# Two transformer blocks on one core: the modulation weights load through GpSimd's DMA queue instead of the sync engine's

## The chip, the core and the metric

The kernel runs on one NeuronCore of a Trainium2 chip. A core has TensorE for matrix products, VectorE (DVE in the profile) and ScalarE (ACT) for element-wise work, GpSimd (POOL), and the sync engine (SP). Each has its own instruction queue, and they wait for each other only through semaphores. Transfers between the chip's memory (HBM) and the on-chip buffer run on 16 DMA engines. They are issued from the queue of the sync engine, of ScalarE or of GpSimd. The metric is the device time of one execution in microseconds; less is better.

## What is computed

A sequence of 256 tokens of width 2048 goes through two blocks in float32. The first is a mixer layer (RG-LRU, mLSTM and block attention side by side) with cross attention to a memory of 256 tokens. The second has two layers, a pooling branch and a latent attention branch (MLA), both modulated by two condition vectors. What matters here is this modulation, and that everything else is products with large weights, each used once:

```python
for i in range(DEPTH_2):                       # 2 layers
    shift, scale, gate = jnp.split(jax.nn.silu(c) @ ada_w[i] + ada_b[i], 3, axis=-1)
    h_lat = rms_norm_2(x, pre_norm[i]) * (1 + scale[:, None]) + shift[:, None]
    shift_c, scale_c, gate_c = jnp.split(jax.nn.silu(c_ctx) @ ada_w[i] + ada_b[i], 3, axis=-1)
    h_ctx = rms_norm_2(ctx, pre_norm[i]) * (1 + scale_c) + shift_c
    ...
    x = x + gate[:, None] * rms_norm_2(y_lat, post_norm[i])
```

`ada_w` is 2 x 2048 x 6144 in float32, 100 MB of the 307 MB that the kernel reads. It is multiplied with two vectors only, and none of it depends on the tokens.

## The kernel before

**The weight products.** Every weight product is an object `Product`: a weight in *chunks* of 512 rows by up to 512 columns (`KC` = 4 row tiles of 128, 1 MB), in column groups. There are 196 chunks in all. A chunk goes through four hands: the sync engine loads it into one of two buffers `raw` (`sp_chunk`, L253), ScalarE rounds it into a high part (`act_high`, L302, `w_high`), VectorE subtracts that from it into a low part (`dve_low`, L312, `w_low`), and TensorE multiplies high and low parts with the operand (`pe_chunk`, L497 to L499 for one sequence of 256 columns, L506 to L508 for two sequences, 512 columns). 48 matrix instructions belong to a full chunk. Buffers are in pairs, so chunk c + 2 may be loaded once VectorE has made the low part of chunk c (`lo_ready`).

**The modulation weights.** `ada_w` is loaded in 192 *units* of 512 rows by 256 columns, 512 KB each and 1 KB a row, into one of two buffers `ada_raw` (`sp_unit`, L267). VectorE multiplies a unit with both condition vectors and adds it up in `ada_acc` (`dve_ada`): eight instructions a unit, one for each of 4 row tiles and 2 vectors, L427, or L423 for the first two of a block. Four units are a block; then TensorE collects the sums (`pe_ada`, L441 or L444), and VectorE waits for that before it overwrites them. Unit u + 2 may be loaded when unit u is summed: the issue waits for `ada_link`, which every one of the eight instructions raises.

**How units are spread.** The units have no own place in time. They are handed out to the chunks of some products (the dictionary `ada`), so that VectorE sums them while TensorE multiplies:

```python
ada = {kv: 1, win_a: 1, win_c: 1, mixo: 1, xq: 1, xo: 1, po: 2}
ada.update({p: 1 for p in pu})
ada.update({p: 2 for p in pgate + uq + ukv})
```

`kv`, `win_a`, `win_c`, `mixo`, `xq` and `xo` are products of one sequence with one unit a chunk, 80 units. The `pu` products have two sequences and one unit a chunk, 16 units. The four `pgate` products and `po` have two sequences and two units a chunk, 64 units. The last 32 units belong to the *pairs*, the eight pairs of attention heads of the MLA layer (`uq0` and `ukv0` to `uq7` and `ukv7`, two units each). `win_b`, `cq`, `mg01`, `ckv`, `kr`, `mg23` (together the stage `latents` with the operands' normalisation) and the last product `mo` have none. In `dve_product` and its like the order on VectorE is: low part of chunk j, what the former group left, units of chunk j, low part of chunk j + 1.

**The sync engine's queue** is what the change touches. `sp_group` issues chunk j, then the units of chunk j, then chunk j + 1. Each issue waits at its place, and everything behind it waits too. Ahead of the first product stand the four loads of the memory tokens (`sp_turn`, L611). For the pairs `sp_pairs` has a written-out order. GpSimd has no work in the kernel. The kernel's head reserves 1024 bytes of each partition for descriptors of GpSimd's transfers: `nc = bacc.Bacc("TRN2", target_bir_lowering=False, num_devices=1, dynamic_dma_scratch_size=1024)`. ScalarE's queue issues some thirty small loads of vectors at the start, and the tokens of the other inputs.

The stages follow each other with a wait of all three compute engines for one another (`stage_end`, L790).

Of the kernel before, what the change touches and what calls it, by code (L numbers as in the profile page):

```python
# [21 lines left out]
DEBUG_STOP = None  # L22
# [102 lines left out]
def build(nc, a, out):  # L125
# [24 lines left out]
    uq = [Product(f"uq{j}", mw_uq, 1, 1, 3, 1, "copy1", half=1, width=384, pack="heads", col0=384 * j, dest=Q_SETS[j % 2], banks=4)  # L150
          for j in range(8)]
    ukv = [Product(f"ukv{j}", mw_ukv, 1, 1, 4, 2, "copy2", src="ps", col0=GW * j, dest=KV_SETS[j % 2], banks=4) for j in range(8)]
    mo = Product("mo", mw_out, 4, 4, 4, 1, "gain1", dest=32, banks=6)
    pool_chain = [pu[3], pu[2], pg[3], pu[1], pg[2], pu[0], pg[1], pgate[3], pg[0], pgate[2], pgate[1], pgate[0], po]
    products = [kv, win_a, win_b, win_c, mixo, xq, xo] + pool_chain + [cq, mg01, ckv, kr, mg23]
# [16 lines left out]
    with ctx:  # L172
        def sb(name, shape, dt=F32):
            return ctx.enter_context(nc.sbuf_tensor(name, shape, dt))

        def sem(name):
            return ctx.enter_context(nc.semaphore(name))
# [14 lines left out]
        ARAW = sb("ada_raw", [P, 2, KC, 256])  # L192
# [5 lines left out]
        for name, _, n in VEC:  # L198
            if at % P + n > P:
                at += P - at % P  # L200
            V[name], place[name] = PV[:, at:at + n], at
            at += n
# [18 lines left out]
        ada_loaded = [sem("ada_loaded0"), sem("ada_loaded1")]  # L221
        ada_summed, rows_moved, rows_turned = sem("ada_summed"), sem("ada_rows_moved"), sem("ada_rows_turned")
        rows_added = sem("ada_last_rows_added")
        ada_link = sem("ada_link")
# [16 lines left out]
        block = ctx.enter_context(nc.Block())  # L241


        def sp_chunk(sp, p, i, j):
            c, w = p.chunk0 + j, p.chunks * i
            if isinstance(i, int):
                c, w = c + w, 0
            slot = c % 2
            if c >= 2 or not isinstance(i, int):
                sp.wait_ge(lo_ready, c + w - 1)  # L250
            rows = p.w[p.korder[j] * KC * P:(p.korder[j] + 1) * KC * P, :]
            src = rows.rearrange("(k p) n -> p k n", p=P)[:, :, bass.ds(p.col0 + p.stride * i, p.width)]
            sp.dma_start(RAW[:, slot, :, 0:p.width], src).then_inc(raw_ready[slot], 16)  # L253

        def sp_unit(sp, p, i, j, q):
            u0 = p.unit0 + p.ada * j + q
            uw = p.ada * p.chunks * i
            if isinstance(i, int):
                u0, uw = u0 + uw, 0
            part, us = u0 % 4, u0 % 2  # L260
            if u0 >= 2 or not isinstance(i, int):
                sp.wait_ge(ada_link, 8 * (u0 + uw - 1))
            b = u0 // 4
            layer, col = b // 24, (b % 24) * 256
            src = a["ada_w_2"][layer, part * KC * P:(part + 1) * KC * P, :]
            src = src.rearrange("(k p) n -> p k n", p=P)[:, :, bass.ds(col, 256)]
            sp.dma_start(ARAW[:, us], src).then_inc(ada_loaded[us], 16)  # L267

        def sp_group(sp, p, i):
            for j in range(p.chunks):  # L270
                sp_chunk(sp, p, i, j)
                for q in range(p.ada):
                    sp_unit(sp, p, i, j, q)

        def packed(p):

# [249 lines left out]
        def sp_product(sp, p):  # L526
            sp_group(sp, p, 0)
            if p.groups > 1:
                for g in range(1, p.groups):
                    sp_group(sp, p, g)  # L530
# [77 lines left out]
        def sp_turn(sp, q, src):  # L608
            for part in range(4):
                cols = slice(512 * part, 512 * (part + 1))  # L610
                sp.dma_start(tok(q)[:, :, cols], src[:, cols].rearrange("(a p) f -> p a f", p=P)).then_inc(tok_in[part], 16)  # L611
# [1429 lines left out]
        def sp_pairs(sp):  # L2041
            sp_chunk(sp, uq[0], 0, 0)
            sp_chunk(sp, ukv[0], 0, 0)
            for j in range(8):
                if j < 7:
                    sp_chunk(sp, uq[j + 1], 0, 0)
                sp_unit(sp, uq[j], 0, 0, 0)
                if j < 7:
                    sp_chunk(sp, ukv[j + 1], 0, 0)
                sp_unit(sp, uq[j], 0, 0, 1)  # L2050
                sp_unit(sp, ukv[j], 0, 0, 0)
                sp_unit(sp, ukv[j], 0, 0, 1)


        out_t, out_c = sem("out_turned"), sem("out_copied")
# [60 lines left out]
        def sp_out(sp):  # L2116
            for n in range(8):
                k4, h = n // 2, n % 2
                sp.wait_ge(out_c, n + 1)
                sp.dma_start(out[0, h * P:(h + 1) * P, 512 * k4:512 * (k4 + 1)],  # L2120
                             OUTT[:, h, 512 * k4:512 * (k4 + 1)]).then_inc(out_done, 16)
            sp.wait_ge(out_done, 16 * 8)
# [34 lines left out]
        @block.sync  # L2157
        def _(sp):
            sp_turn(sp, 0, a["mem"][0])
            sp_product(sp, kv)  # L2160
            for p in products[1:3]:
                sp_product(sp, p)
            if DEBUG_STOP:
                lim = STAGES.index(DEBUG_STOP)
            else:
                lim = len(STAGES)
            for p in products[3:]:
                if p in uq[1:] + ukv:
                    continue
                stage = ("pools" if p in pool_chain else "latents" if p in (cq, mg01, ckv, kr, mg23) else "pairs" if p is uq[0]  # L2170
                         else stage_of.get(p.name, p.name))
                if STAGES.index(stage) >= lim:
                    break
                if p is uq[0]:
                    sp_pairs(sp)
                    continue
                sp_product(sp, p)
            if not DEBUG_STOP:
                sp_out(sp)

        @block.scalar
        def _(act):
# [154 lines left out]
```

## Time and profile before

| | |
|---|---|
| runs shown | 2194.4, 2195.2, 2198.5 us; median 2195.2 |
| profiled execution | 2198.2 us, span 2196.4 us |
| TensorE busy | 1864.9 us, 85% of the span |
| VectorE busy | 1521.2 us, 69% |
| ScalarE busy | 778.0 us, 35% |
| GpSimd busy | 0.2 us |
| read from HBM | 307.2 MB, 141 GB/s over the span |
| transfers of the sync engine's queue | 303.6 MB, 42.2% of 16 engines' span |
| granted TensorE clock | 0.907 of full speed on average |

The profiled execution is one of its own, 3.0 us above the median of the runs. In the profile a line such as L267 is a line of the kernel. `SPq` is the sync engine issuing transfers: the time there is that of the issue, and the landing is given apart. A wait of an engine is put down to what came last before it went on.

### The profile page before, as it was taken

The page shows a single profiled execution, that of the slowest core. Times are in us where ns is not written, and L with a number is a line of the kernel's source. Part 1 is how long each engine was busy: PE and PEld are TensorE (multiplying, and loading weights), DVE is VectorE, ACT ScalarE, POOL GpSimd, SP SyncE. Part 2 cuts the span into 40 slices and gives each one's busy share as a digit, 9 for nine tenths or more (in the row PEclk, how much of TensorE's full clock was granted, in tenths as well). Part 3 has the DMA queues.
Part 4 walks back from the last instruction along what each step waited for, and adds up shares of the span by engine and source line. Part 5 has one row for each costly group of instructions (what it writes and reads, how often), then busy time and mean ns, then how long its engine had stood idle before and what let it go on. Part 6 is the DMA issues. An engine that isn't in the chain of part 4 may idle for free.

```text
span 2196.4 us, 27206 instructions
## 1 busy us (share of the span) xinstructions
PE 1864.9 (85%) x10672; PEld 1582.7 (72%) x10672; DVE 1521.2 (69%) x2851; ACT 778.0 (35%) x1048; POOL 0.2 (0%) x4
## 2 busy tenths in 40 slices
PE   3969960769979967569999999999688989999797
PEld 2969950559958966458888877777587886666497
DVE  3778966378858866468668787978765277887444
ACT  4343342223333243532233222222443344444243
POOL 0000000000000000000000000000000000000000
PEclk8979975669989987879999999999799999999798
DMA  3748830038735734024445444555243343342153
GB/s 122 250 127 257 262 112 1 1 95 264 254 102 189 252 115 142 31 97 134 134 135 167 159 154 153 192 172 185 85 137 102 122 153 125 106 139 82 66 174 115
DMA packets 214780, 311.10 MB, mean 142 GB/s; under 512 B 11528, under 2 KB 118392, under 8 KB 214652
## 3 DMA queue, kind: packets, MB, share of 16 engines
q1 hardware_dynamic: 207104, 303.59, 42.2%
q10 hardware_dynamic: 7548, 5.78, 0.9%
q8 instruction: 84, 1.38, 0.3%
q14 instruction: 44, 0.36, 0.1%
HBM read 307.23 MB, written 2.10 MB: 141 GB/s over the span
## 4 chain that ended last, share of the span: by engine, by line
PE 53%; DVE 11%; ACT 3%; issue 1%; DMA 0%; DVEq 0%; ACTq 0%
PE bank L506 10%; PE bank L507 10%; PE bank L508 10%; PE bank L497 5%; PE bank L499 5%; PE bank L498 5%; DVE ada_acc L427 3%; DVE w_low L312 2%; PE bank L1838 2%; ACT w_high L302 2%; PE bank L672 2%; PE bank L1837 1%; PE bank L441 1%; DVE big L700 1%; PE bank L1857 1%
## 5 line engine op out<-in xcount | busy, mean ns | idle before, releaser
L497 PE MATMUL bank<-operand,w_high 128*128 128x256 f32 x2000 | 583.7, 292 | 80.3 <-DVEq L790 55.0
L312 DVE TENSOR_TENSOR w_low<-raw,w_high 128x2048 fp32r<-128x2048 f32 (+4 forms) x208 | 437.2, 2107 | 271.6 <-ACT w_high L302 269.7
L302 ACT ACTIVATE w_high<-raw 128x2048 fp32r<-128x2048 f32 (+4 forms) x208 | 366.0, 1765 | 645.0 <-PE bank L499 274.0
L427 DVE SCALAR_TENSOR_TENSOR ada_acc<-ada_raw,silu_c,ada_acc 128x256 f32<-128x256 f32 x1440 | 584.0, 482 | 1.8 <-DMA ada_raw<-in_ada_w 0.5
L498 PE MATMUL bank<-operand,w_high 128*128 128x256 f32 x2000 | 575.4, 288 | 0.0
L499 PE MATMUL bank<-operand,w_low 128*128 128x256 f32 x2000 | 575.1, 288 | 0.0
L497 PEld LDWEIGHTS bank<-operand,w_high 128*128 128x128 f32 x2000 | 394.0, 197 | 103.1 <-ACTq L790 45.2
L498 PEld LDWEIGHTS bank<-operand,w_high 128*128 128x128 f32 x2000 | 394.1, 197 | 0.1
L499 PEld LDWEIGHTS bank<-operand,w_low 128*128 128x128 f32 x2000 | 393.5, 197 | 0.0
L506 PE MATMUL bank<-operand,w_high 128*128 128x512 f32 x784 | 309.7, 395 | 29.7 <-DVEq L790 28.3
L507 PE MATMUL bank<-operand,w_high 128*128 128x512 f32 x784 | 307.0, 392 | 0.0
L508 PE MATMUL bank<-operand,w_low 128*128 128x512 f32 x784 | 306.4, 391 | 0.0
L506 PEld LDWEIGHTS bank<-operand,w_high 128*128 128x128 f32 x784 | 148.1, 189 | 69.4 <-ACTq L790 28.7
L508 PEld LDWEIGHTS bank<-operand,w_low 128*128 128x128 f32 x784 | 148.0, 189 | 31.4
L507 PEld LDWEIGHTS bank<-operand,w_high 128*128 128x128 f32 x784 | 148.2, 189 | 30.2
L506 PE MATMUL bank<-operand_small,w_high 128*128 128x512 f32 x256 | 103.6, 405 | 3.5 <-DVE big L406 3.5
L508 PE MATMUL bank<-operand_small,w_low 128*128 128x512 f32 x256 | 100.4, 392 | 0.0
L507 PE MATMUL bank<-operand_small,w_high 128*128 128x512 f32 x256 | 100.4, 392 | 0.0
L346 ACT ACTIVATE big<-bank 128x256 f32<-128x256 f32 x91 | 34.6, 380 | 98.8 <-PE bank L499 98.1
L672 PE MATMUL bank<-big,ones 128*128 128x256 f32 x192 | 52.6, 442 | 16.8 <-ACT big L651 16.8
L506 PEld LDWEIGHTS bank<-operand_small,w_high 128*128 128x128 f32 x256 | 48.5, 189 | 18.6 <-DVE w_low L312 5.3
L672 PEld LDWEIGHTS bank<-big,ones 128*128 128x128 f32 x192 | 42.8, 226 | 25.5 <-issue 10.0
(296 smaller groups left out, 1619.7 us busy)
## 6 DMA issues: line engine op xcount, KB each, us to landing
ada_raw<-in_ada_w SPq DMA_DIRECT2D x192, 512.0 KB, 3.9
raw<-in_w_in SPq DMA_DIRECT2D x48, 1024.0 KB, 5.1
raw<-in_pool_w_in SPq DMA_DIRECT2D x32, 1024.0 KB, 5.6
raw<-in_mla_w_in SPq DMA_DIRECT2D x24, 1024.0 KB, 5.1
raw<-in_w_out SPq DMA_DIRECT2D x16, 1024.0 KB, 5.8
raw<-in_pool_w_out SPq DMA_DIRECT2D x16, 1024.0 KB, 6.2
raw<-in_mla_w_out SPq DMA_DIRECT2D x16, 1024.0 KB, 5.1
raw<-in_xa_wkv SPq DMA_DIRECT2D x8, 1024.0 KB, 6.9
```

The lines of the kernel that those rows point to most:

```text
L302: ins = nc.scalar.activation(view(HI, slot, False), view(RAW, slot, True), ACT.Copy)
L312: ins = nc.vector.tensor_sub(view(LO, slot, False), view(RAW, slot, True), view(HI, slot, False).bitcast(F32))
L346: nc.scalar.activation(dest_ap(p, i, n), PB[p.bank[i, n]][:, 0:T], ACT.Copy).then_inc(act_freed, 1)
L427: ins = nc.vector.scalar_tensor_tensor(ACC[:, v], ARAW[:, us, k], SC[:, v, part * KC + k:part * KC + k + 1], ACC[:, v], ALU.mult, ALU.add)
L497: pe.matmul(bank[:, 0:T], pick(HI), x[:, 0, :], start=first, stop=False, skip_group_check=True)
L498: pe.matmul(bank[:, 0:T], pick(HI), x[:, 1, :], start=False, stop=False, skip_group_check=True)
L499: ins = pe.matmul(bank[:, 0:T], pick(LO), x[:, 0, :], start=False, stop=last, skip_group_check=True)
L506: pe.matmul(bank[:, :], pick(HI), x[:, 0, :], start=first, stop=False, skip_group_check=True)
L507: pe.matmul(bank[:, :], pick(HI), x[:, 1, :], start=False, stop=False, skip_group_check=True)
L508: ins = pe.matmul(bank[:, :], pick(LO), x[:, 0, :], start=False, stop=last, skip_group_check=True)
L672: ins = pe.matmul(PB[5][:, 0:T], ones[:, :], BIG[:, SQ0 + 4 * (s % 2) + k, :], start=(s == 0 and k == 0), stop=(s == n["nk"] // 4 - 1 and ...
L1838: la_pe.inc(pe.matmul(bank[:, :], BIG[r, q_of(a)[2], qt * P:(qt + 1) * P], KRT[r, :], start=False, stop=True), "s", a, u)
```

## The change

The units' loads leave the sync engine's queue and go to GpSimd's, in the same order, with the same waits for `ada_link` and the same landing semaphores. GpSimd does nothing else. The sync engine's queue keeps the chunks. Nothing is changed on TensorE, VectorE and ScalarE.

```diff
--- before.py
+++ after.py
@@ -252,25 +252,23 @@
             src = rows.rearrange("(k p) n -> p k n", p=P)[:, :, bass.ds(p.col0 + p.stride * i, p.width)]
             sp.dma_start(RAW[:, slot, :, 0:p.width], src).then_inc(raw_ready[slot], 16)
 
-        def sp_unit(sp, p, i, j, q):
+        def pool_unit(pool, p, i, j, q):
             u0 = p.unit0 + p.ada * j + q
             uw = p.ada * p.chunks * i
             if isinstance(i, int):
                 u0, uw = u0 + uw, 0
             part, us = u0 % 4, u0 % 2
             if u0 >= 2 or not isinstance(i, int):
-                sp.wait_ge(ada_link, 8 * (u0 + uw - 1))
+                pool.wait_ge(ada_link, 8 * (u0 + uw - 1))
             b = u0 // 4
             layer, col = b // 24, (b % 24) * 256
             src = a["ada_w_2"][layer, part * KC * P:(part + 1) * KC * P, :]
             src = src.rearrange("(k p) n -> p k n", p=P)[:, :, bass.ds(col, 256)]
-            sp.dma_start(ARAW[:, us], src).then_inc(ada_loaded[us], 16)
+            pool.dma_start(ARAW[:, us], src).then_inc(ada_loaded[us], 16)
 
         def sp_group(sp, p, i):
             for j in range(p.chunks):
                 sp_chunk(sp, p, i, j)
-                for q in range(p.ada):
-                    sp_unit(sp, p, i, j, q)
 
         def packed(p):
 
@@ -2044,12 +2042,8 @@
             for j in range(8):
                 if j < 7:
                     sp_chunk(sp, uq[j + 1], 0, 0)
-                sp_unit(sp, uq[j], 0, 0, 0)
                 if j < 7:
                     sp_chunk(sp, ukv[j + 1], 0, 0)
-                sp_unit(sp, uq[j], 0, 0, 1)
-                sp_unit(sp, ukv[j], 0, 0, 0)
-                sp_unit(sp, ukv[j], 0, 0, 1)
 
 
         out_t, out_c = sem("out_turned"), sem("out_copied")
@@ -2178,6 +2172,16 @@
             if not DEBUG_STOP:
                 sp_out(sp)
 
+        @block.gpsimd
+        def _(pool):
+            for p in products:
+                if DEBUG_STOP:
+                    break
+                for i in range(p.groups):
+                    for j in range(p.chunks):
+                        for q in range(p.ada):
+                            pool_unit(pool, p, i, j, q)
+
         @block.scalar
         def _(act):
             for name, st in all_steps:
```

What stands in the queues where the prediction looks: first the sync engine's, before the change, at the start of `po` (`in_pool_w_out`; `in_ada_w` are the units).

```order
L253 DMA raw<-in_pool_w_in 128x4x512 [waits lo_ready]
L267 DMA ada_raw<-in_ada_w 128x4x256 [waits ada_link] x2
L253 DMA raw<-in_pool_w_out 128x4x512 [waits lo_ready]
L267 DMA ada_raw<-in_ada_w 128x4x256 [waits ada_link] x2
L253 DMA raw<-in_pool_w_out 128x4x512 [waits lo_ready]
L267 DMA ada_raw<-in_ada_w 128x4x256 [waits ada_link] x2
```

And the same queue before, where the pairs begin (`in_mla_w_uq` and `in_mla_w_ukv` are the chunks of `uq` and `ukv`):

```order
L267 DMA ada_raw<-in_ada_w 128x4x256 [waits ada_link] x2
L253 DMA raw<-in_mla_w_in 128x4x512 [waits lo_ready] x16
L253 DMA raw<-in_mla_w_in 128x4x64 [waits lo_ready] x4
L253 DMA raw<-in_mla_w_in 128x4x512 [waits lo_ready] x8
L253 DMA raw<-in_mla_w_uq 128x4x384 [waits lo_ready]
L253 DMA raw<-in_mla_w_ukv 128x4x512 [waits lo_ready]
L253 DMA raw<-in_mla_w_uq 128x4x384 [waits lo_ready]
L267 DMA ada_raw<-in_ada_w 128x4x256 [waits ada_link]
L253 DMA raw<-in_mla_w_ukv 128x4x512 [waits lo_ready]
L267 DMA ada_raw<-in_ada_w 128x4x256 [waits ada_link] x3
L253 DMA raw<-in_mla_w_uq 128x4x384 [waits lo_ready]
L267 DMA ada_raw<-in_ada_w 128x4x256 [waits ada_link]
```

The sync engine's queue with the change, from the last `pgate` products to the pairs:

```order
L253 DMA raw<-in_pool_w_in 128x4x512 [waits lo_ready] x12
L253 DMA raw<-in_pool_w_out 128x4x512 [waits lo_ready] x16
L253 DMA raw<-in_mla_w_in 128x4x512 [waits lo_ready] x16
L253 DMA raw<-in_mla_w_in 128x4x64 [waits lo_ready] x4
L253 DMA raw<-in_mla_w_in 128x4x512 [waits lo_ready] x8
L253 DMA raw<-in_mla_w_uq 128x4x384 [waits lo_ready]
L253 DMA raw<-in_mla_w_ukv 128x4x512 [waits lo_ready]
L253 DMA raw<-in_mla_w_uq 128x4x384 [waits lo_ready]
L253 DMA raw<-in_mla_w_ukv 128x4x512 [waits lo_ready]
L253 DMA raw<-in_mla_w_uq 128x4x384 [waits lo_ready]
```

The units are gone from between the chunks; at the pairs they had stood behind chunks of `uq1` and `ukv1`. GpSimd's queue with the change, whole:

```order
L2331 MEMSET const-float32-0.0 128x1
L2331 MEMSET const-float32-1.0 128x1
L2331 MEMSET const-bfloat16-1.0 128x1
L2331 MEMSET const-uint8-127 128x1
L2175 UNCONDITIONAL_BRANCH [waits barrier_Pool_Activation_PE_DVE_SP_gather]
L267 DMA ada_raw<-in_ada_w 128x4x256 x2
L267 DMA ada_raw<-in_ada_w 128x4x256 [waits ada_link] x190
L172 UNCONDITIONAL_BRANCH
```

All 192 units stand there in a row; only the first two wait for nothing.

## Rows read from the trace of the kernel before

**Rows 1.** The page: the span, busy us, share and instructions of each engine
```profile
span 2196.4 us, 27206 instructions
...
PE 1864.9 (85%) x10672; PEld 1582.7 (72%) x10672; DVE 1521.2 (69%) x2851; ACT 778.0 (35%) x1048; POOL 0.2 (0%) x4
```

**Rows 2.** TensorE's waits: us in total, times, longest
```profile
PE bank L753 <- DMA small<-in_ml_bf: 18.4, 1, 18.4
PE bank L497 <- DVE w_low L312: 18.4, 10, 4.2
...
PE bank L444 <- DVE ada_acc L427: 3.2, 1, 3.2
```

**Rows 3.** Busy us by stretch: inside `win_a`, `mixo` and `po`
```profile
core 0: us, PE busy (x) PEld busy (x) DVE busy (x) ACT busy (x) POOL busy (x), PEclk, DMA share, GB/s
150.00:280.00 130.00, 130.00 (x1057) 126.42 (x1056) 116.94 (x196) 47.25 (x42) 0.00 (x0) 1.00 0.79 251
...
680.00:755.00 75.00, 75.00 (x606) 72.63 (x606) 69.44 (x124) 23.53 (x13) 0.00 (x0) 1.00 0.78 253
...
1400.00:1540.00 140.00, 140.00 (x610) 111.73 (x609) 113.16 (x222) 38.60 (x48) 0.00 (x0) 1.00 0.55 188
```

**Rows 4.** Chunk loads in 150:280, inside `win_a`: xcount, ns, first and last start
```profile
L253 SPq DMA_DIRECT2D raw<-in_w_in x22: 367/368/368, 151.2 to 278.0; - x22
```

**Rows 5.** The unit buffer, whole span: xcount, ns min/median/max, first and last start
```profile
L427 DVE SCALAR_TENSOR_TENSOR ada_acc<-ada_raw,silu_c,ada_acc x1440: 474/481/503, 55.0 to 2043.4; 128x256 f32<-128x256 f32 x180
L267 SPq DMA_DIRECT2D ada_raw<-in_ada_w x192: 367/368/2982, 4.0 to 2033.5; - x192
...
DMA to landing us min/median/max: 3.4/3.9/13.0
```

**Rows 6.** The unit buffer in 1404:1527, inside `po`
```profile
L267 SPq DMA_DIRECT2D ada_raw<-in_ada_w x22: 367/368/368, 1405.1 to 1525.8; - x22
...
  PE bank L441: 18.2, 5
...
DMA to landing us min/median/max: 3.8/3.9/5.0
```

**Rows 7.** The sync engine's queue at the start of `po`: start, us, instruction
```profile
1349.70 0.51 SPq L253 DMA_DIRECT2D raw<-in_pool_w_out  x1
1376.93 3.54 SPq L267 DMA_DIRECT2D ada_raw<-in_ada_w  x2
1380.51 0.51 SPq L253 DMA_DIRECT2D raw<-in_pool_w_out  x1
```

**Rows 8.** ScalarE's waits for chunks, whole span: us, times, longest
```profile
ACT w_high L302 <- DMA raw<-in_pool_w_out: 46.1, 5, 18.5
ACT w_high L302 <- DMA raw<-in_pool_w_in: 40.1, 4, 12.1
```

**Rows 9.** VectorE in `po`, in order of time
```profile
1484.17 5.63 DVE L427 SCALAR_TENSOR_TENSOR ada_acc<-ada_raw,silu_c,ada_acc 128x256 f32<-128x256 f32 x14
1489.71 2.29 DVE L312 TENSOR_TENSOR w_low<-raw,w_high 128x2048 fp32r<-128x2048 f32 x1
1491.92 6.43 DVE L427 SCALAR_TENSOR_TENSOR ada_acc<-ada_raw,silu_c,ada_acc 128x256 f32<-128x256 f32 x16
```

**Rows 10.** The chain that ended last, at the start of the pairs: start, us, what
```profile
1804.64 3.27 DVE ada_acc L427 x8
...
1807.92 3.69 DMA ada_raw<-in_ada_w
...
1811.64 3.27 DVE ada_acc L427 x8
...
1814.95 1.06 PE bank L444 x4
```

**Rows 11.** The sync engine's queue in the first 22 us
```profile
0.73 2.36 SPq L611 DMA_DIRECT2D big<-in_mem  x4
...
6.36 2.98 SPq L267 DMA_DIRECT2D ada_raw<-in_ada_w  x1
```

## Prediction

> **What bounds the kernel now.** I read the page first, then TensorE's waits, then the busy time of single stretches, then the two weight buffers, and last the chain of waits where the pairs begin. The page has TensorE busy for 85% of the span and GpSimd with nothing to do [rows 1]. Inside the weight products TensorE does not pause at all: 130.00 of 130.00 us in `win_a`, 75.00 of 75.00 in `mixo`, 140.00 of 140.00 in `po`, at a granted clock of 1.00 [rows 3]. So there a load can only cost time, not give any back. What VectorE has free is little: 13 of 130 us in `win_a`, 5.6 of 75 in `mixo`, 27 of 140 in `po`. TensorE's waits for a weight's low part are 18.4 us in ten places, and one wait of 3.2 us is for a modulation sum [rows 2]. No wait of TensorE names a chunk or unit load.
>
> A unit lands 3.9 us after its issue in the middle case, 3.4 at best, 13.0 at worst (the first ones) [rows 5]. VectorE needs 8 instructions of some 0.4 us step for a unit, 3.27 us together [rows 10].
>
> **The change, part by part.**
>
> *Taken from the sync queue: 192 issues of 0.37 us* [rows 5]. In the 1-sequence products a chunk goes out every (278.0 - 151.2) / 21 = 6.04 us [rows 4]. Its issue waits for the low part of the chunk two before; the unit issues ahead of it wait for sums that VectorE makes before that low part. So the chunks don't go out earlier there: 0 us. In the products with two units a chunk the queue does hold chunks back. At the start of `po` the sync engine issues a chunk at 1349.70, stands until 1376.93 before the next pair of units, and issues the next chunk at 1380.51 [rows 7]. ScalarE waits 46.1 and 40.1 us for such chunks [rows 8]. The change takes most of these 86 us away, and I cost that at 0: TensorE is busy for every microsecond of that stretch [rows 3], and VectorE and ScalarE only prepare the next chunk sooner. What is late next is TensorE itself.
>
> *Added: 192 loads on GpSimd's queue.* GpSimd waits for nothing but the unit buffer, and nothing else is queued on it. The cost is a unit's latency there, which this trace does not show. From below it is the best unit load of the sync queue, 3.4 us; from above, the 6.2 us that I get when the median load first waits out a VectorE subtraction of 2.29 us [rows 5, 9]. I take 4.4, the median 3.9 and one more issue time of 0.5 [rows 7], since it is the same transfer on the same DMA engines. By the Trainium skill, "DMA: Bandwidth & Descriptors", section "Anatomy of one DMA — SWDGE (gpsimd) path", such a load takes 2.0 us and its bytes at 436 GB/s, which for 512 KB makes 3.2 us, an estimate from that page alone; by it the term of the pairs, below, would be 2 x 3.2 - 7.0 = -0.6 us. The second unknown is how many loads GpSimd's queue holds. The sync queue takes two in a row [rows 7]. The kernel reserves only 1024 bytes of a partition for GpSimd's descriptors, so I take one at a time, and two as the other end.
>
> *Where the latency is covered.* In the 1-sequence products a buffer comes free when a unit is summed, and its successor is due two chunks later less one sum: 2 x 6.04 - 3.27 = 8.8 us against 4.4. One load per chunk also fits one at a time, as long as it takes under 6.04. In `po` the sequence is unit, unit, low part (2.29), unit, unit [rows 9]. A load is due 3.2 + 2.3 = 5.5 us after its request. With 4.4 the first of a pair is in time, and the second, which starts when the first has landed, comes 2 x 4.4 - 3.2 = 5.6 after its own request: VectorE waits 0.1 us. That vanishes in the 18.2 us which VectorE waits there for TensorE at five block starts [rows 6]. Sum: 0.
>
> *Where it is not covered: the start of the pairs* [rows 10]. The first two units there land long before use (the sync queue gave them only at the end of `latents`). The third is requested at 1804.6 when the first is summed, the fourth at 1807.9. Now the chain runs 1807.92 + 3.69 us of load, then 3.27 us of sums, then TensorE at 1814.95, which had waited 3.2 us [rows 2]. With 4.4 us, one at a time, the third lands at 1809.0, the fourth at 1813.4, and its sums end at 1816.7: 1.8 us later. With two in flight it is 1812.3 + 3.3 = 1815.6: 0.7 us later. In later pairs steps of the attention stand between the sums on VectorE, and all four loads stay covered.
>
> *The start of the kernel.* The first two unit loads now stand behind 2 MB of tokens and two chunks [rows 11]; from GpSimd they compete from the first microsecond. TensorE's first work waits for the small vectors at 18.4 us [rows 2], which end together with all this traffic. The bytes are the same, so 0. The two units are 1 MB of some 6, a sixth of 18 us, so the ends are 3 us either way.
>
> **Sum:** 0 + 0 + 0 + 1.8 + 0 = +1.8 us. The profiled execution took 2198.2 us, 3.0 above the median of the runs shown; from it I get 2200.0, from the median 2195.2 + 1.8 = 2197.0. A measurement of this kernel can tell about 0.2%, 4.4 us, from no change.
>
> **The rivals.**
>
> *GpSimd's loads are slow (slower, 15%).* In `po` a unit is due every (1525.8 - 1405.1) / 21 = 5.75 us [rows 6]. With one load at a time this is the point from which it decides: a latency above 5.75 makes the loads the bound of the 32 chunks with two units (64 units), and above 6.04 of the 80 units of the 1-sequence products too. At 6.0 us it costs 64 x 0.25 = +16 us (2211); at the 6.2 of a load that waits out a subtraction 64 x 0.45 + 80 x 0.16 = +42 (2237); at 6.5, 64 x 0.75 + 80 x 0.46 = +85 (2280). For it: loads beside chunks are slower on the sync queue too, up to 5.0 in `po` [rows 6]. Against it: the median there is 3.9, so GpSimd would have to add half again. The Trainium skill bears on it, in "SBUF — State Buffer", sections "SBUF: two separate sides" and "Who interferes with whom": GpSimd cannot write descriptors while VectorE holds the port pair they share. By that page a subtraction of two tensors takes only the read side and does not starve them; no row here shows either.
>
> *VectorE itself is slowed by GpSimd (slower, 10%).* In `win_a` VectorE has 13 us free for 21 units, in `mixo` 5.6 for 10: about 0.6 us a unit. Only what a load takes beyond that reaches TensorE. With 1.0 us it is 80 x 0.4 = +32 us (2229); with one blocked sum of 0.48 us nothing. Nothing in the trace speaks for it, as GpSimd is idle.
>
> *A middling latency (10%).* Between 5.0 and 5.75 us each second unit in `po` and the gates comes 1.3 to 2.8 us late. Blocks mostly absorb it; I price it with the pairs (2 x 5.5 - 7.0 = +4.0) at +3 to +8 us (2198 to 2203).
>
> *The earlier requests pay (5%).* Units and chunks that no longer wait for each other cut the kernel's start by up to 3 us and some of the 18.4 us of waits for low parts [rows 2]: -5 us, 2190. Against it: most of those ten waits lie in products without units.
>
> **How the numbers follow.** The forecast, loads absorbed but for 1.8 us, has 60%. The range takes in it (2194 to 2200), the early gain's near part, the middling latency and the low ends of both slow rivals: 2192 to 2213 leaves out about 0.2. Slower by over 0.2% is 0.15 + 0.10 and most of the middling case, 0.32; faster 0.05; the same 0.63.
>
> **What would show it.** In the profile of the changed kernel: GpSimd's queue with 192 loads and a median to landing near 4.4 us; the sync queue without its stands; ScalarE's 86 us of waits for chunks nearly gone; TensorE still busy for all of the three stretches; at the pairs, the fourth sum's end 1 to 2 us later relative to its first. A median above 5.75, waits of VectorE for units in `win_a`, or sums longer than 0.48 us each would show the forecast wrong.

## The result, and the profile after

| | before | after | ratio |
|---|---|---|---|
| median, 10 runs each | 2195.83 us (2194.38 to 2198.54) | 2201.38 us (2196.8 to 2203.28) | 1.0024 [1.0014, 1.0034] |
| profiled execution | 2198.22 us, span 2196.4 | 2201.21 us, span 2199.4 | |

The change makes the kernel slower by 0.24%, about 5.3 us. The forecast was 2197.0 us, +1.8 against the median shown then. The range of 2192 to 2213 us holds the result, but the case given the highest chance, no change beyond 0.2%, was missed by a little. The two profiled executions lie only 3.0 us apart, because that of before was 2.4 us above its median.

The page of the changed kernel first: the span, the engines, and two of the lines on DMA queues. The last row is of the page of before.

```profile
span 2199.4 us, 27206 instructions
...
PE 1868.2 (85%) x10672; PEld 1585.6 (72%) x10672; DVE 1520.9 (69%) x2851; ACT 778.3 (35%) x1048; POOL 145.0 (7%) x196
...
q1 hardware_dynamic: 105728, 202.91, 28.0%
q0 software_dynamic: 27648, 100.68, 14.0%
```

```profile
q1 hardware_dynamic: 207104, 303.59, 42.2%
```

VectorE and ScalarE do the same work [rows 1]. GpSimd is now busy for 145 us, all of it issuing. The columns of the queue lines are packets, MB, and the share of 16 engines' time. The 100.68 MB of the units took 207104 - 105728 = 101376 packets (1 KB each) on the sync engine's queue and take 27648 (3.6 KB on average) on GpSimd's.

The unit buffer over the whole span, in the changed kernel (answers to [rows 5]):

```profile
L425 DVE SCALAR_TENSOR_TENSOR ada_acc<-ada_raw,silu_c,ada_acc x1440: 469/477/487, 55.4 to 2044.9; 128x256 f32<-128x256 f32 x180
L267 POOL DMA_DIRECT2D ada_raw<-in_ada_w x192: 748/753/887, 1.3 to 2035.4; - x192
...
  DMA ada_raw<-in_ada_w: 24.2, 16
...
DMA to landing us min/median/max: 3.8/4.3/8.1
```

A unit lands 4.3 us after its issue in the middle case; 4.4 was taken. A sum takes 477 ns at the median (481 before), so VectorE is not slowed by GpSimd. New is the third line: VectorE stands 24.2 us, in 16 places, for units that haven't landed. In the three stretches TensorE is still busy throughout (answers to [rows 3]; columns as there):

```profile
150.00:280.00 130.00, 130.00 (x1057) 126.42 (x1056) 115.80 (x192) 46.77 (x41) 15.82 (x21) 1.00 0.79 256
680.00:755.00 75.00, 75.00 (x607) 72.66 (x606) 69.71 (x124) 23.00 (x12) 9.04 (x12) 1.00 0.77 250
1400.00:1540.00 140.00, 140.00 (x611) 111.68 (x610) 109.76 (x217) 38.71 (x48) 18.58 (x25) 1.00 0.56 181
```

The waits of the changed kernel that answer to [rows 2, 8] (us in total, times, longest):

```profile
ACT w_high L300 <- DMA raw<-in_w_in: 29.2, 7, 4.9
ACT w_high L300 <- DMA raw<-in_w_out: 26.1, 6, 5.0
PE bank L751 <- DMA small<-in_ml_bf: 18.7, 1, 18.7
PE bank L495 <- DVE w_low L310: 16.6, 10, 4.2
PE bank L442 <- DVE ada_acc L425: 5.1, 1, 5.1
PE bank L439 <- DVE ada_acc L425: 3.7, 1, 3.7
```

ScalarE's 86 us of waits for `pool_w_out` and `pool_w_in` chunks are gone, as forecast. Other chunks are waited for instead, those of the one-sequence products. TensorE's wait for a sum at the pairs has grown from 3.2 to 5.1 us. The last line is a second wait of TensorE for a sum. The prediction counted one such wait in the kernel before, but there were two. Its rows left this one out:

```profile
PE bank L441 <- DVE ada_acc L427: 4.2, 1, 4.2
```

**Where it is.** The chain of waits runs through both places. This is the chain of before at the start of `po`, then that of after at the same place:

```profile
1379.99 2.50 DVE operand L931 x4
1382.48 2.83 DVE ada_acc L427 x8
1385.56 3.27 DVE ada_acc L427 x8
1388.87 1.49 PE bank L441 x4
```

```profile
1374.33 3.27 DVE ada_acc L425 x8
1377.60 1.94 issue
1379.54 4.36 DMA ada_raw<-in_ada_w
1383.92 3.27 DVE ada_acc L425 x8
1387.24 1.94 PE bank L439 x4
```

Before, VectorE makes the four sums of `po`'s first block one after the other, and TensorE waits for the last. After, the chain passes through a load and through 1.94 us in which GpSimd could have issued but did not. VectorE in the changed kernel shows what that costs:

```profile
1379.91 3.25 DVE L425 SCALAR_TENSOR_TENSOR ada_acc<-ada_raw,silu_c,ada_acc 128x256 f32<-128x256 f32 x8
1383.92 3.26 DVE L425 SCALAR_TENSOR_TENSOR ada_acc<-ada_raw,silu_c,ada_acc 128x256 f32<-128x256 f32 x8 [0.77 <-DMA ada_raw<-in_ada_w]
```

At the pairs the same thing happens (the chain of after; answers to [rows 10]), with GpSimd's own timeline below it:

```profile
1804.05 3.26 DVE ada_acc L425 x8
1807.31 1.60 issue
1808.91 4.00 DMA ada_raw<-in_ada_w
1812.94 3.27 DVE ada_acc L425 x8
1816.25 1.94 PE bank L442 x4
```

```profile
1804.53 0.75 POOL L267 DMA_DIRECT2D ada_raw<-in_ada_w  x1 [254.64 <-DVE ada_acc L425]
1808.91 0.76 POOL L267 DMA_DIRECT2D ada_raw<-in_ada_w  x1 [3.63 <-issue]
```

The fourth unit's buffer is free at 1807.31, but its load starts at 1808.91. The third unit landed at 1808.6, 0.3 us earlier. So one load is in flight at a time here, as the prediction took it, and by issue and landing no two of the 192 loads overlap in this profile. From the start of the second unit's sums (1804.05) to the end of the fourth's (1816.21) it is 12.16 us. Before it was 1804.64 to 1814.91, 10.27 us [rows 10]. The difference is 1.9 us, and 1.8 was forecast. The match is partly luck. The two loads took 4.1 and 4.0 us, less than the 4.4 that was taken. But each also starts late: the third unit's 0.4 us after its buffer was free, the fourth's 0.3 us after the third landed. Neither delay was in the sum. Together it is 8.8 us, as 2 x 4.4.

So the one priced term was right, and yet 5.3 us are measured. The open question for the runs is what the other 3.5 us are.

### The profile page after: what moved, and what is told of

Its sections match the earlier page's. It is cut to its first block, busy times and chain, and to the rows that moved or that the text cites. A ratio compares the mean times of both kernels' runs of the same rounds, so it can differ in the third digit from the quotient of the medians.

```text
span 2199.4 us, 27206 instructions
## 1 busy us (share of the span) xinstructions
PE 1868.2 (85%) x10672; PEld 1585.6 (72%) x10672; DVE 1520.9 (69%) x2851; ACT 778.3 (35%) x1048; POOL 145.0 (7%) x196
## 3 DMA queue, kind: packets, MB, share of 16 engines
q1 hardware_dynamic: 105728, 202.91, 28.0%
q0 software_dynamic: 27648, 100.68, 14.0%
## 4 chain that ended last, share of the span: by engine, by line
PE 54%; DVE 10%; ACT 3%; issue 2%; DMA 1%; DVEq 0%; ACTq 0%
PE bank L504 10%; PE bank L505 10%; PE bank L506 10%; PE bank L495 5%; PE bank L496 5%; PE bank L497 5%; DVE ada_acc L425 2%; DVE w_low L310 2%; PE bank L1836 2%; ACT w_high L300 1%; PE bank L670 1%; PE bank L1835 1%; PE bank L439 1%; PE bank L1855 1%; DVE big L698 1%
## 5 line engine op out<-in xcount | busy, mean ns | idle before, releaser
L425 DVE SCALAR_TENSOR_TENSOR ada_acc<-ada_raw,silu_c,ada_acc 128x256 f32<-128x256 f32 x1440 | 584.7, 478 | 25.5 <-DMA ada_raw<-in_ada_w 24.2
L267 POOL DMA_DIRECT2D ada_raw<-in_ada_w x192 | 144.8, 754 | 1890.9 <-DVE ada_acc L425 1672.6
```

The source lines that it names most:

```text
L267: pool.dma_start(ARAW[:, us], src).then_inc(ada_loaded[us], 16)
L425: ins = nc.vector.scalar_tensor_tensor(ACC[:, v], ARAW[:, us, k], SC[:, v, part * KC + k:part * KC + k + 1], ACC[:, v], ALU.mult, ALU.add)
```

## The experiments

Two theories. **W:** the cost is TensorE's waits for modulation sums where four of them follow each other, and comes from one load at a time. **C:** it is spread over the one-sequence products, whose chunk loads became slower. The expectations below also use the letter P for W's place at the pairs. They speak of a wait at "the end of `po`". That was misread: by the chain above it is at `po`'s start, in its first block. Ratios are to the kernel before on the same chip.

**1. The change once more, unaltered, and 2. with more space for descriptors.**

> The changed kernel once more, unaltered, to see which differences of the two profiles repeat. Theory P (the cost sits at the pairs: loads of units come one at a time, so the fourth sum of the pairs is late): the kernel is 4 to 6 us above the one before, TensorE's wait for the fourth sum is about 5.1 us again (3.2 before), and the step of +2 us at the start of the pairs is there again. Theory C (the cost is spread over the one-sequence products, where chunk loads got slower beside GpSimd's units, 6.4 to 6.9 us instead of 5.1 to 5.8): the time is the same, but small steps stand in win_a, win_c and mixo, and TensorE's waits for low parts grow. Steps of the first comparison that are noise (about -2.4 at the start of the gates, +1.4 at po, -3.0 and +2.4 in the latents) change size or sign here.

Measured: 2202.30 us, ratio 1.0030 [1.0018, 1.0041]. TensorE's waits for sums are 5.0 us at `po` and 4.9 at the pairs; in this order they are given for the other runs too. The differences of 1 to 3 us that the expectation called noise did change sign or size, and waits for low parts are 19.3 us (18.4 before).

```diff
-dynamic_dma_scratch_size=1024
+dynamic_dma_scratch_size=1536
```

> Only the space for GpSimd's descriptors grows, from 1024 to 1536 bytes of a partition. Theory 1 (the space holds one unit's descriptors, so the next load waits for the landing of the last): with half as much again there is at best part of a second unit in flight; if it holds two, no load starts 0.31 us after a landing, VectorE's waits for units fall from 24 us to under 8, the fourth sum of the pairs is 1 us earlier and the kernel 1 us shorter than the changed one. Theory 2 (GpSimd's queue takes one transfer at a time whatever the space): nothing moves, VectorE waits 24 us again, the time is 5 us above the kernel before.

Measured: 2197.10 us, ratio 1.0008 [0.9999, 1.0016]. GpSimd at the pairs in this run, and the waits for units and sums of the whole span, TensorE's first:

```profile
1801.43 0.76 POOL L267 DMA_DIRECT2D ada_raw<-in_ada_w  x1 [259.37 <-DVE ada_acc L425]
1804.60 0.75 POOL L267 DMA_DIRECT2D ada_raw<-in_ada_w  x1 [2.41 <-DVE ada_acc L425]
```

```profile
  PE bank L442: 3.9, 1
...
  PE bank L439: 2.8, 1
  DVE ada_acc L425: 1.2, 1
...
DMA to landing us min/median/max: 3.8/4.2/9.8
```

The second load starts 3.17 us after the first, while that is still in flight, and the releaser is VectorE's sum and no longer "issue". VectorE's 24.2 us of waits for units fall to 1.2. With the latency nearly the same (4.2 against 4.3 us), two loads in flight take away about two thirds of the loss. Theory 1 stands: it was the space for descriptors, and theory 2 falls.

**3. and 4. The pairs apart.** The units of some products go back to the sync engine's queue at their old places. They raise semaphores of their own there (`ada_loaded_sp`). Only `on_pool` differs between these runs; it is shown for run 3, and run 4 has `p in uq + ukv`:

```diff
+        on_pool = lambda p: p not in uq + ukv
-            pool.dma_start(ARAW[:, us], src).then_inc(ada_loaded[us], 16)
+            pool.dma_start(ARAW[:, us], src).then_inc((ada_loaded if on_pool(p) else ada_loaded_sp)[us], 16)
```

> The 32 units of the pairs go back to the sync engine's queue at their old places, the other 160 stay with GpSimd. Theory P (the cost sits at the pairs): 0 to +1.5 us against the kernel before, TensorE's wait for the fourth sum 3.2 us again. Theory C (it is spread over the one-sequence products): still +3 to +4 us, and only the 2 us of the pairs' start go.

Measured: 2198.21 us, ratio 1.0012 [1.0003, 1.0021]. Waits 6.3 and 3.8 us. The wait at `po` is long because in this profile TensorE's clock did not fall ahead of it, so that TensorE comes to it sooner.

> The reverse: only the 32 units of the pairs go through GpSimd, the other 160 are issued by the sync engine as before. Theory P: +4 to +5 us against the kernel before. Theory C: +2 us, the late fourth sum alone.

Measured: 2198.17 us, ratio 1.0015 [1.0006, 1.0024]; the wait at the pairs is 5.2 us, at `po` 4.2. So the 32 units of the pairs alone cost 1.5/1000 or 3.3 us, where the late sum explains 1.9; without them 2.6 us remain. Neither theory is right as it stood: P had the whole cost at the pairs, C only 2 us of it.

**5. and 6. The other units apart**, with `on_pool` true for `(kv, win_a, win_c, mixo, xq, xo)` in 5, for `pu + pgate + [po]` in 6.

> Only the 80 units of the one-sequence products (kv, win_a, win_c, mixo, xq, xo) go through GpSimd; the 112 others stay with the sync engine. There is one unit a chunk here, so one load at a time is enough. Theory W (what the change costs is TensorE's waits for modulation sums at the end of po and at the pairs): same time as the kernel before, within 1 us, waits for sums 4.2 and 3.2 us as before. Theory C (chunk loads slowed by GpSimd's units cost time): +1 to +3 us; chunk loads of win_a and win_c take 6.4 to 7 us instead of 5.1 in either theory.

Measured: 2196.58 us, ratio 1.0005 [0.9997, 1.0014]. Waits 2.8 and 3.5 us.

> Only the 80 units of the gates and po (pu, pgate, po) go through GpSimd. Theory W: TensorE's wait for the last sums of po grows from 4.2 us to 5 or 6, the wait at the pairs stays at 3.2; the time is +1 to +2 us against the kernel before. Theory C: the same as before, since chunk loads of these products did not get slower (5.4 to 6.2 us in both).

Measured: 2198.07 us, ratio 1.0009 [1.0000, 1.0018]. The wait at `po` is 4.8 us, at the pairs 3.7. The three parts add up: 0.5 + 0.9 + 1.5 = 2.9 thousandths, against 2.4, 3.0 and 1.7 for the whole change in three comparisons. The 80 units of the one-sequence products, where one load a chunk needs no second one in flight, are the cheapest share and can't be told from nothing, though their chunk loads are slower there too. Chunk loads in 150:280 of this run:

```profile
DMA to landing us min/median/max: 4.9/6.2/7.6
```

The same line reads 4.4/5.0/7.2 for before and 4.2/6.7/8.0 for after. In the other runs with these units on GpSimd's queue it is 6.1 to 7.0 us. So C's fact is true and its cost is at most small: by the interval of this run, not above 1.4 thousandths.

**7. Each unit as two transfers of 256 KB, space left at 1024 bytes.**

```diff
-            pool.dma_start(ARAW[:, us], src).then_inc(ada_loaded[us], 16)
+            for h in range(2):
+                pool.dma_start(ARAW[:, us, 2 * h:2 * h + 2], src[:, 2 * h:2 * h + 2]).then_inc(ada_loaded[us], 16)
-                dve.wait_ge(ada_loaded[us], 16 * (u0 // 2 + 1) + 8 * uw)
+                dve.wait_ge(ada_loaded[us], 32 * (u0 // 2 + 1) + 16 * uw)
```

> The changed kernel with each unit as two transfers of 256 KB on GpSimd's queue, the space for descriptors left at 1024 bytes. If the space holds a number of descriptors and a whole unit takes over half of it, three halves fit: half of the next unit is in flight beside the last one, VectorE's waits for units fall from 20 to 24 us to under 10, and the time lies 1 to 3 us below the changed kernel. If a queue of GpSimd takes one transfer at a time, a unit takes two transfers in a row, some 6.5 us together, more than the 5.75 us in which one is due in po: +20 us or more.

Measured: 2197.62 us, ratio 1.0010 [1.0002, 1.0019]. GpSimd at the pairs:

```profile
1802.76 1.44 POOL L268 DMA_DIRECT2D ada_raw<-in_ada_w  x2 [257.85 <-DVE ada_acc L426]
1805.93 0.72 POOL L268 DMA_DIRECT2D ada_raw<-in_ada_w  x1 [1.73 <-DVE ada_acc L426]
1807.13 0.73 POOL L268 DMA_DIRECT2D ada_raw<-in_ada_w  x1 [0.48 <-issue]
```

Two halves go out together, then the third when the buffer is free, and the fourth waits 0.48 us for space. VectorE's waits for units are 9.1 us. So it isn't that the queue takes one transfer at a time: what is limited is how much is outstanding. A second kernel without the larger space confirms run 2, at twice the issues.

**8. Slow loads by hand.** The rival with the highest price, made by asking late, with no other work.

```diff
-                pool.wait_ge(ada_link, 8 * (u0 + uw - 1))
+                pool.wait_ge(ada_link, 8 * (u0 + uw - 1) + (4 if p.ada == 2 else 0))
```

> The changed kernel, but in the products with two units a chunk GpSimd asks for a unit only when four of the eight sums of the unit before it are made: 1.64 us later for 96 units, with no other work added. This is the rival of slow loads by hand. It says: a unit is then due every 0.4 + 4.4 + 1.6 = 6.4 us in po against the 5.75 it may take, 0.65 us over for 64 units, about +42 us; with what VectorE had free at block starts, +20 to +42. If the waits of VectorE at block starts swallow it, under +10.

Measured: 2286.29 us in one run, +90 us. The unit buffer in 1430:1560, inside `po`:

```profile
L267 POOL DMA_DIRECT2D ada_raw<-in_ada_w x19: 748/751/760, 1432.8 to 1555.4; - x19
...
  DMA ada_raw<-in_ada_w: 41.9, 18
...
DMA to landing us min/median/max: 4.2/4.4/5.1
```

A unit goes out every (1555.4 - 1432.8) / 18 = 6.8 us, not 6.4, because a low part often stands between the two sums it waits for. Against the 5.75 us of [rows 6] that is 1.06 us for each of the 32 units of `po`, 34 us; the trace has `po` 36 us longer than the kernel before, and 34 longer than the change in its first profile. Against the kernel before the gates are 25 us longer, and the pairs with the start of `mo` 29, which the expectation had left out. So a spacing above the 5.75 us costs what the rival says, the excess times the units. The expectation was too low twice: with 0.65 us a unit for 1.06, and by stopping at `po`. VectorE's free time at block starts swallows nothing of this.

**9. and 10. Both kernels again**, for the profiles.

> The kernel before, unaltered, as a second profile and as a comparison with itself. Ratio 1.000 within 0.001. TensorE's waits for modulation sums should be 4.2 and 3.2 us again, whereas the stretches in which its clock is granted at half speed should shift: if this profile has as much matrix work at half clock as the profiles of the variants (196 to 205 us) and not as they stand against the first profile (204), stages' differences of 1 to 3 us with equal waits are placed by the clock and not by the change.

Measured: 2195.04 us, ratio 1.0002 [0.9993, 1.0011]. Waits 4.2 and 3.9 us.

> The changed kernel a third time, beside the kernel before on this chip. Theory W: ratio 1.002 to 1.003; waits for sums at the end of po 3.7 to 5.0 us (4.2 before) and at the pairs 4.9 to 5.1 us (3.2 before), and the half-speed stretch behind the pairs' wait is 6.8 us long again, against 3.4 us in every variant in which that wait was 4.2 us or less. If it is 3.4 us here, the clock's part of the cost at the pairs is chance.

Measured: 2200.19 us, ratio 1.0017 [1.0008, 1.0025]. Waits 4.9 and 5.1 us.

**11. and 12. Towards a version below both.** Both have 1536 bytes; `on_pool` is that of run 6 in the first, that of run 3 in the second.

> An attempt at a version below both: the 80 units of the gates and po through GpSimd, with 1536 bytes for descriptors, all others by the sync engine. Theory W: the wait at the end of po falls from 4.2 to 2.8 us as in the run with the larger space, the pairs wait 3.2 to 3.7; -1.4 us, so 0.9985 to 1.0 of the kernel before, at the limit of what can be told. If sums that come earlier in po are worth nothing, 1.000 to 1.001.

Measured: 2195.77 us, ratio 1.0005 [0.9997, 1.0014]. Waits 4.2 and 3.4 us.

> The changed kernel with both remedies: 1536 bytes for descriptors, and the 32 units of the pairs by the sync engine. Theory W: no exposed wait is longer than before (2.8 at po, 3.2 to 3.8 at the pairs), so 0.999 to 1.0005 of the kernel before. If something else that goes with GpSimd's loads costs the rest (chunk loads of 6.4 to 7 us in the one-sequence products), 1.001 as in the run with the larger space alone.

Measured: 2196.36 us, ratio 0.9999 [0.9990, 1.0007]. Waits 4.2 and 3.9 us. Its chunk loads in the one-sequence products are waited for as in the change (ScalarE, 48.9 us for `in_w_in`), and it is as fast as before, to 0.7 thousandths by the interval. That ends theory C as an explanation. No version beats the kernel before: the 2.8 us at `po` that runs 2 and 5 showed is no gain, as the next table says.

**All profiles side by side.** The length of `po` and of the first exposed step of the pairs is that between the semaphore steps that tell a chunk as finished: the last of the gates to the last of `po`, and `ukv0`'s to `uq1`'s. "Busy" is TensorE's share of it.

| run | units by GpSimd, one at a time | `po` us (busy) | pairs step us (busy) |
|---|---|---|---|
| before | none | 195.17 (187.42) | 13.77 (10.53) |
| before again | none | 195.13 (187.37) | 14.37 (10.52) |
| one_seq_by_gpsimd | neither here nor there | 195.19 (188.90) | 13.96 (10.48) |
| ring_1536 | two at a time | 195.19 (188.90) | 14.39 (10.50) |
| half_units | more than one | 195.17 (187.40) | 14.77 (10.53) |
| gates_gpsimd_ring | two at a time in `po` | 195.17 (187.43) | 13.89 (10.48) |
| pairs_sync_ring | two at a time in `po` | 195.16 (187.42) | 14.43 (10.52) |
| two_seq_by_gpsimd | in `po` | 195.63 (187.27) | 14.24 (10.50) |
| pairs_by_sync | in `po` | 196.82 (186.99) | 14.33 (10.54) |
| pairs_by_gpsimd | in the pairs | 195.13 (187.41) | 15.97 (10.80) |
| after | in both | 197.29 (190.12) | 15.85 (10.72) |
| after again | in both | 195.87 (187.36) | 16.57 (11.63) |
| after, third | in both | 195.65 (187.19) | 16.76 (11.64) |

`po` is 195.13 to 195.19 us long in eight profiles, whatever TensorE's clock did in it, and 195.63 to 197.29 in the five with one load at a time: 1.1 us more on average. The pairs' step averages 14.1 us where the sync engine loads the pairs' units, and 16.3 in the four with one load at a time: 2.1 us more. No profile of one group lies in the other. The sum is 3.2 us. Where the wait at `po` was only 2.8 us (one_seq_by_gpsimd, ring_1536), TensorE was busy 1.5 us longer ahead of it at its lower clock, and the stage is as long as ever.

Both differences have two parts. At `po` TensorE goes on 28.45 us after the last chunk of the gates in all eight profiles, and 29.0 to 29.3 in the five: 0.5 to 0.9 us later, which is how long VectorE waits for the unit. In three of the five that is all. At the pairs TensorE goes on 6.0 to 6.6 us after `ukv0`'s chunk in the seven profiles, and 7.7 to 7.9 in the four: 1.45 us later on average. The rest in both places is the clock.

**The clock's share.** TensorE's granted clock after the pairs' wait, 10 us from the sums' collection on, in the second profile of after and then in the second of before (us, busy PE, PEld, DVE, ACT, POOL, PEclk, DMA share, GB/s):

```profile
1815.40:1825.40 10.00, 10.00 (x35) 5.97 (x36) 4.18 (x7) 3.47 (x6) 0.76 (x1) 0.71 0.18 58
```

```profile
1811.00:1821.00 10.00, 9.98 (x38) 5.73 (x39) 5.25 (x9) 4.29 (x7) 0.00 (x0) 0.83 0.01 2
```

With the shorter wait (3.9 us) 0.83 is granted, with the longer (4.9) 0.71: (0.83 - 0.71) x 10 = 1.2 us of work at full speed, and the busy column of the table has 1.1 more. The first profile of before has 0.83 too, and the third of after 0.71. The stretch at the lower level (1.2 GHz) at this wait is 3.4 us long in the nine profiles where the wait is 3.2 to 4.2 us, and 6.8 us in the four where it is 4.9 to 5.2. Even so the busy column has only 0.2 to 0.3 more in `after` and pairs_by_gpsimd: there the low stretch began some 3 us before TensorE went on, and fell in part on the wait itself. So the surcharge in the step is seen in two profiles of four. In these other two the chunk ahead of the step also took 10.0 and 9.1 us instead of 7.6, at the lower clock. The wait behind it can't have caused that. Whether the change did stays open.

At `po` the same is seen in two of the five, `after` and pairs_by_sync, whose stage is 2.1 and 1.7 us longer instead of 0.5 to 0.7. The 10 us from the sums' collection on, in the first profile of after and then in the third:

```profile
1387.20:1397.20 10.00, 9.96 (x31) 7.20 (x32) 10.00 (x20) 1.92 (x1) 1.51 (x2) 0.69 0.54 180
```

```profile
1387.50:1397.50 10.00, 9.97 (x37) 7.36 (x38) 10.00 (x20) 1.92 (x1) 1.51 (x2) 0.84 0.55 182
```

In the two the low stretch at this wait is 6.8 us long, in the other eleven 3.4. The length of the wait alone doesn't decide it. It was 3.7 and 6.3 us in the two, and 4.8 to 5.0 in the three that kept 3.4. What does decide is not shown.

## Why the prediction was right and wrong

- **Latency 4.4 us:** measured 4.3 from the issue on. What comes before the issue was left out: GpSimd's queue starts 0.40 us after the buffer is free, the sync engine's 0.03. The rule of the Trainium skill that was weighed against it ("DMA: Bandwidth & Descriptors", section "Anatomy of one DMA — SWDGE (gpsimd) path"; 3.2 us for 512 KB as an estimate from that page) is not borne out here: the best of 192 loads took 3.8 us.
- **One load at a time:** right, and the cause of most of the loss, since with two in flight the ratio falls from 1.0017 to 1.0030 to 1.0008.
- **Start of the pairs, +1.8 us:** the sums end 1.9 us later relative to the first. With two at a time +0.7 was forecast; the wait there is 3.9 us against the 3.2 and 3.9 of before, so 0 to 0.7. The term was undersized all the same. The step of the pairs is 2.1 us longer on average, 1.45 because TensorE goes on later and 0.7 because it then works longer at its lower clock. The clock was not in the sum.
- **`po`, "Sum: 0": the step that failed.** The arithmetic said that VectorE waits 0.1 us for each second unit and that this "vanishes in the 18.2 us which VectorE waits there for TensorE at five block starts". It waited 0.5 to 0.8 us in `po`'s first block in all five profiles, and there nothing absorbs it, because TensorE waits for that block's sums. The stage is 1.1 us longer on average, 0.7 by the late sum and 0.4 by the clock. The other waits were absorbed, though they were larger than priced: of VectorE's 24.2 us for units in the first profile 7.4 lie in the gates up to 1345 and 10.2 in `po` from 1400 on, and the gates' 32 chunks take 362.5 us in every profile but that of run 8. Three choices hid this. The window of [rows 3] began at 1400, after the place. Of TensorE's waits for sums [rows 2] quoted the one of 3.2 us and not the one of 4.2 us at L441. And the price was taken from a steady stretch, while `po` begins with the sums of four units and no low part between them, only an operand step of 2.50 us. The chain of waits of the kernel before passed through it, at 1385.56 and 1388.87.
- **Issues taken from the sync queue, 0 us:** right. The 86 us of ScalarE's waits went and TensorE's stretches did not move. But the reason given, that TensorE is busy throughout "that stretch", was read from 1400 on, while the sync engine's stand of [rows 7] ends at 1376.93. TensorE does stop there, for 3.5 us, and in all profiles alike, for VectorE's work on the gates' results.
- **Start of the kernel, 0 with 3 us either way:** not told apart. The stretch to `kv`'s last chunk is 104.2 to 106.3 us in the three profiles of after, 104.9 and 103.7 in the two of before.
- **Rivals.** Slow loads: didn't come, the median is 1.4 us below the knee; run 8 shows that a spacing above it costs the excess times the units, in the pairs too, which its price left out. VectorE slowed by GpSimd: didn't come, 477 ns against 481. By "SBUF — State Buffer", section "Who interferes with whom" (the Trainium skill), a subtraction of two tensors doesn't keep GpSimd from its descriptors; the trace agrees, as the 99 issues that fell beside a low part's subtraction took 748 to 765 ns, and all 192 took 748 to 887. Middling latency, +3 to +8 us, with the late second units mostly absorbed by blocks: the measured size, and partly the mechanism, came from this side, but at 4.3 us of latency and not above 5.0.
- **The sum.** Forecast +1.8, measured about +5.3 (3.1 to 7.5 by the interval; +3.7 and +6.6 in the two later comparisons). Two places hold 3.2 us. The other 2 or so are not located. TensorE's time at its lower clock differs from profile to profile by more than that (196 to 213 us of its busy time), so single profiles can't find them. One step ahead of the gates alone, from the 84th finished chunk to the 85th, takes 80.2, 83.0 and 80.6 us in the three profiles of the changed kernel. Run 5 allows up to 1.4 thousandths for the units of the one-sequence products; whether they cost anything stays open. That the range of 2192 to 2213 held the result is partly luck: it was made wide for rivals that didn't come, and the cost it was to cover, late sums at `po` and the clock, stood in no term of the sum.

## What to carry to other kernels

When loads move to GpSimd's queue, look first at how many it can have in flight, by whether its issue follows the buffer's release or the last landing; here 512 bytes more for descriptors took back some 3 of 5 us. A latency that a steady stretch hides must be priced again where a stage begins: list every wait of the bounding engine for that operand, however short, and choose the windows so that they hold these places. A wait that grows by 1 us can cost 2, if the clock then stays low for longer behind it; here it did so in two of four profiles at the pairs and in two of five at `po`.

## What the runs showed of the hardware that was not expected

- GpSimd issues a 512 KB load in 0.75 us against the sync engine's 0.37, and starts 0.40 us after the buffer's release against 0.03; a load that waited for space starts 0.30 us after the landing of the one before.
- With 1024 bytes reserved, at most one load of 512 KB was outstanding, with 1536 two (the two buffers allow no more), and of 256 KB halves three at 1024.
- GpSimd's queue moves 1 KB rows in packets of 3.6 KB on average, and chunk loads beside it take 6.1 to 7.0 us in `win_a` instead of 5.0. That the packets are the cause wasn't tested.
